# MLA projections packed two heads to a tile, rotary parts of four heads to a tile, and values of all heads made token by token

## What is computed

```python
q  = rmsnorm(c_q, g_cq) @ w_uq       # 768 -> 8 heads x (64 nope + 32 rope)
kv = rmsnorm(c_kv, g_ckv) @ w_ukv    # 256 -> 8 heads x (64 nope + 64 value)
q_rope, k_rope = apply_rope(...)     # k_rope: one 32-wide key for all heads
s = (q_nope @ k_nope.T + q_rope @ k_rope.T) * 96 ** -0.5   # causal mask
o = softmax(s) @ v
y_b = o * silu(b_g)
m = sum over the mixers of sigmoid(merge_b) * (y_b @ w_p_b);  x = x + gate * (m @ w_out)
```

## Time and profile before

| | us |
|---|---|
| median of 3 runs | 1353.59 |
| the profiled execution's own time | 1356.47 |
| its span, first to last instruction | 1354.7 |
| TensorE busy | 1308.1 |
| GpSimd busy | 724.1 |
| VectorE busy | 678.0 |
| ScalarE busy | 645.9 |

### The profile page before, as it was taken

The page is one execution under the profiler, slowest core; times in us unless marked ns, Lnnn a source line. Parts: engine busy times, 40 slices in busy tenths (PEclk is TensorE's granted clock), DMA queues, the critical chain, the costliest instruction groups (busy, mean ns, idle before and its releaser), DMA issues.

```text
span 1354.7 us, 17300 instructions
## 1 busy us (share of the span) xinstructions
PE 1308.1 (97%) x5938; PEld 1036.3 (77%) x5938; DVE 678.0 (50%) x1111; ACT 645.9 (48%) x995; POOL 724.1 (53%) x1495
## 2 busy tenths in 40 slices
PE   5999999999999999999979999999999999999996
PEld 2878887787777777788857888778777777778884
DVE  6766776434564344353355677642355423433333
ACT  3366655434554244354335566554455434444431
POOL 3365456674334554576647555576433454556662
PEclk7999999999999999999989999999999999999998
DMA  9321223342223333242222211233211222232221
GB/s 368 120 85 63 70 72 93 132 133 90 82 83 105 114 98 117 89 136 94 94 70 94 78 63 63 71 111 123 86 62 63 83 89 86 78 102 86 93 94 63
DMA packets 40792, 131.89 MB, mean 97 GB/s; under 512 B 5248, under 2 KB 5376, under 8 KB 39424
## 3 DMA queue, kind: packets, MB, share of 16 engines
q1 hardware_dynamic: 30336, 111.57, 24.3%
q10 hardware_dynamic: 10368, 19.21, 4.8%
HBM read 128.13 MB, written 2.10 MB: 96 GB/s over the span
## 4 chain that ended last, share of the span: by engine, by line
PE 91%; DVE 4%; ACT 3%; POOL 1%; issue 1%; DMA 1%; ACTq 0%; DVEq 0%
PE ps_st L774 23%; PE ps_st L776 23%; PE ps_st L775 23%; PE ps_o L796 5%; PE ps_s L827 3%; PE ps_s L874 2%; PE ps_s L898 2%; PE ps_w L883 1%; PE ps_misc L791 1%; POOL w_lo L646 1%; PE ps_misc L782 1%; PE ps_w L729 1%; DMA cur<-params_cur 1%; PE ps_s L829 1%; PE ps_misc L787 1%
## 5 line engine op out<-in xcount | busy, mean ns | idle before, releaser
L646 POOL TENSOR_TENSOR w_lo<-raw,w_hi 128x128 fp32r<-128x128 f32 x1472 | 711.6, 522 | 589.9 <-ACT w_hi L952 589.7
L774 PE MATMUL ps_st<-h_hi,w_hi 128*128 128x512 f32 x984 | 401.0, 407 | 2.5 <-POOL w_lo L646 2.0
L776 PE MATMUL ps_st<-h_hi,w_lo 128*128 128x512 f32 x984 | 384.2, 390 | 0.0
L775 PE MATMUL ps_st<-h_lo,w_hi 128*128 128x512 f32 x984 | 383.5, 390 | 0.0
L774 PEld LDWEIGHTS ps_st<-h_hi,w_hi 128*128 128x128 f32 x984 | 185.2, 188 | 47.4 <-issue 6.8
L775 PEld LDWEIGHTS ps_st<-h_lo,w_hi 128*128 128x128 f32 x984 | 185.3, 188 | 42.0 <-issue 6.2
L776 PEld LDWEIGHTS ps_st<-h_hi,w_lo 128*128 128x128 f32 x984 | 184.9, 188 | 39.8
L952 ACT ACTIVATE w_hi<-raw 128x1024 fp32r<-128x1024 f32 x184 | 193.3, 1051 | 27.9 <-PE ps_st L776 24.7
L974 ACT ACTIVATE gate_t<-gate_x 128x512 f32<-128x512 f32 x80 | 50.5, 631 | 247.6 <-DVE gate_x L1273 247.5
L1273 DVE TENSOR_SCALAR gate_x<-ps_st 128x512 f32<-128x512 f32 x79 | 54.5, 690 | 220.3 <-PE ps_st L776 219.9
L976 ACT ACTIVATE gate_t<-gate_t,cs 128x512 f32<-128x512 f32 x80 | 57.9, 724 | 2.6
(11 more groups left out here) (283 smaller groups left out, 2003.8 us busy)
## 6 DMA issues: line engine op xcount, KB each, us to landing
raw<-w_stream SPq DMA_DIRECT2D x184, 512.0 KB, 3.4
mod_w<-w_mod ACTq DMA_DIRECT2D x64, 256.0 KB, 2.7
pro_w<-w_mod_first SPq DMA_DIRECT2D x8, 1024.0 KB, 14.0
x<-x_t SPq DMA_DIRECT2D x4, 512.0 KB, 7.4
ret_decay<-decay ACTq DMA_DIRECT2D x2, 1024.0 KB, 4.7
out_t<-o_t SPq DMA_DIRECT2D x8, 256.0 KB, 2.1
raw_extra<-w_stream SPq DMA_DIRECT2D x2, 512.0 KB, 20.1
cs<-cst SPq DMA_DIRECT2D x1, 836.0 KB, 7.5
```

Source lines behind the costliest of these rows:

```text
L646: ins = nc.gpsimd.tensor_tensor(lo[:, r], whole[:, r], hi[:, r].bitcast(F32), ALU.subtract)
L774: nc.tensor.matmul(dst[0:m, :], wh, hi, start=(k == 0), stop=False)
L775: nc.tensor.matmul(dst[0:m, :], wh, lo, start=False, stop=False)
L776: last = nc.tensor.matmul(dst[0:m, :], wl, hi, start=False, stop=(k == nk - 1))
```

## The change

- The 8 items `mla` (8 blocks each) become 4 items `mq` (two heads: nope queries 6 blocks, nope keys 2 blocks), 2 items `mr` (rotary queries of four heads in one tile, 6 blocks) and 1 item `mv` (values of all heads, tokens as output rows: 4 outputs of 2 blocks each, the weights being the moving operand). A layer has 92 items.
- The transposes of `mla_qk` and their copies are gone; `mv` is copied to `v_ones` by ScalarE.
- `mr` is rotated by VectorE out of PSUM: one multiplication on 128 partitions, four on 32 partitions each, which read the other half, and one sum (kept in `sq_sum`). For each `mq` VectorE scales two 64-row slices of it into the query tiles and copies two 64-row slices of keys out of PSUM; ScalarE copies the two query slices.
- `kr_rope` first sets 1024 elements per partition of `v_ones` to one, then multiplies once on 128 partitions and four times on 32, and adds twice on 64. Eight small DMAs more make a table of sines at the start, three more fill the cosines.
- The order: `mr 0`, `mv 0`, `mq 0` between the last merge items; `bg 0` between the scores and the transposes of head 0; behind the scores of blocks 1 and 0 of heads 0 to 7 come `bg 1, mq 1, mr 1, mq 2, bg 2, mq 3, bg 3, rq 0`. Nothing but `mla_pv` stands between scores and transposes of heads 1 to 7.
- The masks of the HGRN2 levels are stored at half width, and `sigma` of the first mixer has a place of its own.

```diff
-    if kind == "mla":
+    if kind == "mq":
         return [(CQT, P, 0, P), (CKT, P, CQT * P, P)]
+    if kind == "mr":
+        return [(CQT, P, 0, P)]
+    if kind == "mv":
+        return [(CKT, CH * P, 0, CH * P)]
...
-    for it in ma[1:-3]:
+    for it in ma[1:-4]:
         item(*it)
-    item("mla", 0)
-    item(*ma[-3])
-    s.append(("mla_qk", 0))
-    item("mla", 1)
-    item(*ma[-2])
+    for it, other in zip(ma[-4:], (("mr", 0), ("mv", 0), ("mq", 0))):
+        item(*it)
+        item(*other)
     item(*ma[-1])
-    item("bg", 0)
+    behind = [("bg", 1), ("mq", 1), ("mr", 1), ("mq", 2), ("bg", 2), ("mq", 3), ("bg", 3), ("rq", 0)]
     for h in range(MLA_HEADS):
         s += [("mla_s", h, 3), ("mla_s", h, 2)]
         if h:
             s.append(("mla_pv", h - 1))
-        if h + 1 < MLA_HEADS:
-            s.append(("mla_qk", h + 1))
         else:
-            s.append(("ret_rope", "rq", 0))
-        if h % 2 == 1 and h + 1 < MLA_HEADS:
-            item("bg", (h + 1) // 2)
+            item("bg", 0)
         s += [("mla_t", h, 3), ("mla_t", h, 2), ("mla_s", h, 1), ("mla_s", h, 0)]
-        item(*(("mla", h + 2) if h + 2 < MLA_HEADS else ("rq", h + 2 - MLA_HEADS)))
+        item(*behind[h])
         s += [("mla_t", h, 1), ("mla_t", h, 0)]
...
+            for q in range(0, P, ROPE // 2):
+                first = P - ROPE // 2 if q % (2 * ROPE) < ROPE else P - ROPE
+                sp.dma_start(sin_mla[q:q + ROPE // 2, :], trig[first:first + ROPE // 2, :]).then_inc(tables_in, 16)
...
+                def values_item(it):
+                    for t in range(CH):
+                        dst = take((it, t))
+                        r = slice(t * P, (t + 1) * P)
+                        for k in range(CKT):
+                            hi, lo = moving("mv", 0, k)
+                            nc.tensor.matmul(dst[:], hi[:, r], wh, start=(k == 0), stop=False)
+                            nc.tensor.matmul(dst[:], hi[:, r], wl, start=False, stop=False)
+                            last = nc.tensor.matmul(dst[:], lo[:, r], wh, start=False, stop=(k == CKT - 1))
+                        done(last, (it, t))
...
-                        if e.new(q_ready, h + 1):
-                            pe.wait_ge(q_ready, e.at(q_ready, h + 1))
+                        if e.new(q_ready, h // 2 + 1):
+                            pe.wait_ge(free[e.bank_of((("mq", h // 2), 0))], e.use(free, (("mq", h // 2), 0)))
+                            pe.wait_ge(free[e.bank_of((("mq", h // 2), 1))], e.use(free, (("mq", h // 2), 1)))
+                            pe.wait_ge(q_ready, e.at(q_ready, h // 2 + 1))
...
+                def mla_rope(t):
+                    V.tensor_tensor(t1[:], t[:], trig[:], ALU.mult)
+                    for a in range(0, P, ROPE):
+                        b = a + ROPE if a % (2 * ROPE) == 0 else a - ROPE
+                        last = V.tensor_tensor(t2[a:a + ROPE, :], t[b:b + ROPE, :], sin_mla[b:b + ROPE, :], ALU.mult)
+                    return last
...
+                    elif kind == "mr":
+                        mla_rope(bank[e.bank_of((it, 0))]).then_inc(free[e.bank_of((it, 0))], 1)
+                        V.tensor_tensor(sq_sum[:], t1[:], t2[:], ALU.add).then_inc(dve_link, 1)
+                    elif kind == "mq":
+                        r = slice(0, NOPE) if j % 2 == 0 else slice(NOPE, P)
+                        V.tensor_scalar(mla_q[NOPE:P, 0, :], sq_sum[r, :], MLA_SCALE, None, ALU.mult)
+                        V.tensor_scalar(mla_q[0:NOPE, 1, :], sq_sum[r, :], MLA_SCALE, None, ALU.mult).then_inc(q_ready, 1)
+                        dve.wait_ge(full[e.bank_of((it, 1))], e.use(full, (it, 1)))
+                        V.tensor_copy(mla_kv[0:NOPE, 0, :], ps[0:NOPE, :])
+                        V.tensor_copy(mla_kv[NOPE:P, 1, :], ps[NOPE:P, :]).then_inc(free[e.bank_of((it, 1))], 1)
...
                     elif kind == "kr_rope":
-                        mla_rope(k_rope, k_rope[NOPE:NOPE + ROPE, :], dve_link)
+                        V.memset(v_ones[:, :, :, 1, :], 1.0)
+                        mla_rope(k_rope).then_inc(dve_link, 1)
+                        V.tensor_tensor(mla_kv[0:NOPE, 1, :], t1[0:NOPE, :], t2[0:NOPE, :], ALU.add)
+                        V.tensor_tensor(mla_kv[NOPE:P, 0, :], t1[NOPE:P, :], t2[NOPE:P, :], ALU.add).then_inc(k_ready, 1)
```

## The result

The changed kernel takes 1376.6 us (median of four runs, 1375.3 to 1377.5), the kernel before 1354.1 in the same job: ratio 1.0155, 95% interval [1.0133, 1.0178]. That is 22.5 us more where 16.1 were forecast. By the spans of the profiled executions it is 20.0.

What follows compares the result with a forecast made beforehand. TensorE's work and waits were taken to bound the kernel. Terms in us: -26.9 + 10.4 + 8.4 + 11.6 + 2.2 + 6.4 + 4.0 = +16.1, so 1369.7; own range 1359 to 1379, 8 in 10 for 1353 to 1386.

Steps and rivals of the forecast that it cites:

- What is saved: On TensorE: 72 fewer matmuls, no value transposes, no waits on the exponentials, fewer item insertions; 26.9 us less.
- mr 1: At head 2, VectorE's rotation delays the copy mla_pv needs; wait 5.2 us, twice, 10.4 us.
- mq: Behind heads 1, 3 and 5, the next head's scores wait 1.4 us for VectorE's key copies, six times, 8.4 us.
- bg: At heads 0, 4 and 6, gates delay ScalarE's copy of block 0; waits of 1.34 and 2.23 us, 11.6 together.
- mr 0: The second output of pa 2 waits for the bank the rotation reads; 1.1 us, twice, 2.2 us.
- kr_rope: Added VectorE work delays gate_x of ma 1, split and w_lo; ma 3 waits 3.2 us, twice, 6.4 us.
- The clock: TensorE's clock falls behind the two waits of 5.2 us only, 2.0 us each, 4.0 us.
- third rival: The clock falls at all 18 new waits: 1402 us, or 1386 if half fall; chance 0.12, whole or in part.
- The first rival: TensorE's own work decides, no wait forms and the kernel is faster: 1326.7 us; chance 0.14, whole or half.
- The second: Rival: gates hold no copy of block 0 and the clock stays up: 1354 us, no change; chance 0.10 with similar balances.
- What was to show it: Signs in the trace after, among them the named waits and TensorE's busy time down by 23 to 27 us.
- terms at their lower bounds: kr_rope 4, mr 0 0, bg 9, mr 1 8, mq 7 and no fall, said to give about +2 to +5 us together.

Runs made afterwards that it cites:

- four moves' kernel: The changed kernel with the edits of Experiment 1, experiment 2, Experiment 3 and Experiment 9, and mq 2's own work ahead of mla_pv of head 2: 1340.9 us.
- experiment 2: The changed kernel with VectorE's rotation work for mr 1 four steps later in its order: 1372.0 us.
- experiment 6: The changed kernel with three of the four 32-row multiplications of mr 1's rotation left out, so its output is wrong: 1371.8 us.
- Experiment 9: The changed kernel with the second key copy of mq 1 to 3 made by ScalarE instead of VectorE: 1374.7 us.
- Experiment 1: The changed kernel with ScalarE's and VectorE's own work for bg 1, 2 and 3 four steps later in their order: 1365.5 us.
- Experiment 3: The changed kernel with the step kr_rope behind item pa 0 instead of behind ma 0: 1368.3 us.
- experiment 12: The changed kernel with the key's rotary tile copied into a free PSUM bank, from which kr_rope's products read it: 1378.2 us.
- after: The changed kernel itself, without any further edit: 1376.6 us.
- Experiments 4 and 5: The changed kernel with unread matmuls added ahead of mla_pv of heads 0, 2, 4 and 6: fp32 in 4, 1402.6 us; in the projections' form in 5, 1371.0 us.
- experiments 7 and 8: 7: the changed kernel with the edits of Experiment 1, experiment 2 and Experiment 3 together, 1350.6 us; 8: the four moves' kernel, 1340.9 us.
- experiments 2, 5, 8 and 10: 10: the changed kernel with the edits of Experiment 1, experiment 2 and Experiment 3, and mq 2's own work ahead of mla_pv of head 2: 1343.5 us.

## Why the forecast came out, and where its terms were off

The budget, all but the start (whose 2.6 us belong to that execution): +22.6 measured, +16.1 forecast.

- **What is saved**: 26.9 forecast. With the waits and falls below, 46.0 us, a net of 22.6 leaves 23.4. The four moves' kernel gives about the same from the other side: in the same stretches it is 14.8 us under before, with 11.0 of waits left that before did not have, and 1.7 of before's waits on `w_lo` gone: 14.8 + 11.0 - 1.7 = 24.1. So this term was some 3 us too large. The 72 matmuls are counted, and the two waits on the exponentials are gone. What is left for transposes and insertions is 4 to 5 instead of 7.6; I took 0.44 a group where the bound said 0.36. A part is also that work starts slower behind a wait: the scores behind `mq 1` take 0.93 us to the next instruction instead of 0.86. Where the rest is, no run tells.
- **`mr 1`**: 10.4 forecast, 10.2 measured; shown by experiments 2 and 6, place, cause and price for each instruction.
- **`mq`**: 8.4 forecast, 8.5 measured. Experiment 9 shows the second copy in it, 0.7 us of each wait.
- **`bg`**: 11.6 forecast, 9.2 measured: 1.19 twice, 2.0 three times, and 0.8 at head 6 of layer 1, where the wait moved to the step of the modulation (1.23 instead of before's 0.41). Experiment 1 shows the gate items as their cause; it takes the 0.8 away as well.
- **`mr 0`**: 2.2 forecast, 1.9 measured.
- **`kr_rope`**: 6.4 forecast, at `ma 3`. The waits are at `pa 0`, an item earlier, and grew by 2.7 in each layer, 5.4 us. The step that failed is the path: I followed `gate_x` to ScalarE's `split` and on to `ma 3`'s weights, and passed over the bank that this same `gate_x` frees, which `pa 0` wants at once; and over GpSimd beside VectorE. Experiment 3 takes both away, and the wait goes; experiment 12 takes GpSimd's part away and 1 us of VectorE's, and 2.9 of 3.95 us stay, by the bank. The chain through `split` to `ma 3` was never the longest.
- **The clock**: 4.0 forecast for two falls. Five came: `pa 0` 2.8 and 1.6 (7.16 us instead of 5.57 in layer 1), `mr 1` 2.7 (with the transposes behind it) and 2.0, `bg 2` of layer 0 1.7: 10.8 us. This is the term that was mis-sized most, by 6.8, and it accounts for the difference to the forecast. That the others cancel is luck: the saving was 3.5 too large, and `bg` and `kr_rope` were 2.4 and 1.0 too dear. 2.0 for one fall was about right (2.2 measured on average, and 1.6 for the fall of the earlier trace rows that I took it from, set against the same place in after), the number was not: I charged none behind `kr_rope`'s waits of over 3 us and none behind those of 2.0. The kernel before could have told of the first: the rows I took from it stop at waits of 1.5 us, and early in its layer 1, outside, the clock is at 0.50 behind waits of 3.15 and 4.28 us (granted clock 0.53 from 693 to 704):

```profile
700.02 0.76 PE L706 MATMUL ps_st<-h_hi,w_hi 128*128 128x512 f32 x1 [4.28 <-DVE h_lo L1589]
```

Of the third rival it took a part: five of eighteen. Experiments 4 and 5 show that it is the idle stretch that brings the fall, and experiment 6 that 3 us of it are enough. The rule of the Trainium skill on the page "TensorE: Matmul & The Clock Gate", section "HAM oscillation — how this bites in real kernels", held in after for its waits of 5.1 us in both layers, for those of 3.95 and 3.11 at `pa 0`, and for one of its three of 2.0.
- The first rival, that TensorE's work decides, fell, but experiments 7 and 8 make it true: 26 to 36 us of the changed kernel's time are the order in which ScalarE and VectorE do their work. The second fell with experiment 1: the gates do hold the copies.
- **What was to show it**: TensorE's busy time went down by 12.4 us and not by 23 to 27, because the falls lengthen what it does by 10.8. And two readings were wrong. The waits of before are not the 6.6 us of the earlier trace rows alone, which left the sum as it was, since the others did not change. And the terms at their lower bounds add up to 28 against 26.9, +1 and not +2 to +5.

What stays open: some 3 us in the term of what is saved, and when a wait of about 2 us brings a fall. In the traces of all the kernels here, from 80 us on, a fall follows 12 of the 25 waits of 1.94 to 2.12 us. It follows every wait of 2.9 us and more but three (3.10 and 3.11 in experiment 2, 3.13 in experiment 6; the last wait of each execution is left out, it has one matmul behind it). Of the waits of 1.1 to 1.6 us it follows 6 of 106, four of them at the place of the earlier trace rows, where all fourteen executions wait 1.4 us. So single runs of one kernel differ: in experiment 1 one took 1363.8 us at a mean clock of 0.982, another 1371.9 at 0.973. Experiments 2, 9 and 12 are therefore read from their waits, with the times as a weaker witness.

## What to carry to other kernels

When a change takes work from the bounding engine and gives it to idle ones, list for each of its new instructions what stands behind it in that engine's queue, and how long TensorE has until it wants it: here some 35 us of waits came from a few instructions at each place, put ahead of copies with at most 2 us of slack, and moving them a few steps back turned +1.6% into -1.1%. Follow everything that a late instruction frees, the bank as well as the data, and take away all that is late at one place before judging either. Price a wait of 3 us or more with a fall of the clock behind it, here some 2 us each, and one of about 2 us with half of that: here every second had one.

## What the runs showed of the hardware

**GpSimd beside VectorE.** A piece of `w_lo` (128x128, both operands in SBUF) takes 0.43 to 0.51 us on GpSimd, 0.96 beside `kr_rope` with both operands in SBUF. Beside the same rotation with one operand in PSUM nothing slows; in the four moves' kernel, beside `mr 0`:

```profile
284.91 7.71 POOL L675 TENSOR_TENSOR w_lo<-raw,w_hi 128x128 fp32r<-128x128 f32 x16 [1.58 <-ACT w_hi L998]
```

16 pieces in 7.71, 0.48 each, and 8 in 3.43 in experiment 12. It works both ways: VectorE's four products took 3.46 us with both operands in SBUF and 2.79 with one in PSUM. The Trainium skill has this, page "SBUF — State Buffer", section "Who interferes with whom": a VectorE instruction with two SBUF inputs contends with a GpSimd instruction that reads SBUF. The trace agrees. The memset of experiment 12, which reads nothing, ran beside the first of these 8 pieces and did not show in their 0.43 us either.

**A fall of the clock costs nearly as much behind 3 us of idle time as behind 5.** From its start to that of the transposes `mla_pv` took 3.83 and 3.93 us behind 2.99 of idle time (experiment 6), 4.40 and 4.18 behind 5.1, and 2.2 behind 0.8 to 0.9 (experiments 2, 5, 8 and 10).

**The same wait brings a fall in one execution and none in the next.** The wait of 1.4 us of the earlier trace rows comes at the same place in the fourteen profiled executions, of before, after and the twelve experiments. The clock fell behind it in four (before, experiments 6, 8 and 9) and stayed up in ten.
